# Gating the expert weights with the token index innermost: products on VectorE, and stored gates transposed and scaled by ScalarE

## What is computed

```python
q = (x_blk @ w_query).reshape(b, t, PEER_HEADS, 2, HALF_KEY)
scores = einsum('bthcd,hcnd->bthcn', q, sub_keys)
top_s, top_i = top_k(scores, PEER_TOPK)
...
gate = softmax(best_s)
u = expert_u[expert_idx]
v = expert_v[expert_idx]
act = gelu(einsum('btd,bthkd->bthk', x_blk, u), approximate=False)
out = einsum('bthk,bthkd->btd', gate * act, v)
```

## Time and profile before

| | before |
|---|---|
| median of the three runs | 1621.19 us |
| lowest, highest | 1617.91, 1624.16 us |
| the profiled execution: time | 1617.6 us |
| its span, first to last instruction | 1615.8 us |
| TensorE matmuls busy | 1460.4 us (90%) |
| GpSimd busy | 951.7 us (59%) |
| VectorE busy | 906.1 us (56%) |
| ScalarE busy | 744.1 us (46%) |

### The profile page before, as it was taken

The page is one execution under the profiler, slowest core; times in us unless marked ns, Lnnn a source line. Parts: engine busy times, 40 slices in busy tenths (PEclk is TensorE's granted clock), DMA queues, the critical chain, the costliest instruction groups (busy, mean ns, idle before and its releaser), DMA issues.

```text
span 1615.8 us, 22681 instructions
## 1 busy us (share of the span) xinstructions
PE 1460.4 (90%) x8920; PEld 1272.1 (79%) x8920; DVE 906.1 (56%) x1521; ACT 744.1 (46%) x1356; POOL 951.7 (59%) x665
## 2 busy tenths in 40 slices
PE   0699899869999599979998998999999999999998
PEld 0378566759988589657998998999998777778886
DVE  4464689245521487642379285777765787842222
ACT  2144212256544466534454555444444554555554
POOL 0063000336766364215689999876665999987675
PEclk8798555689999799989999999999999999999999
DMA  7434225225455243203544544545555566555552
GB/s 267 178 131 165 96 105 205 82 75 177 171 186 194 84 157 105 79 26 131 208 161 157 186 177 163 183 165 174 176 174 197 209 226 231 215 187 204 183 190 97
DMA packets 48298, 261.65 MB, mean 162 GB/s; under 512 B 5440, under 2 KB 14016, under 8 KB 19008
## 3 DMA queue, kind: packets, MB, share of 16 engines
q1 hardware_dynamic: 37984, 249.58, 43.4%
q10 hardware_dynamic: 10208, 10.63, 1.9%
HBM read 250.75 MB, written 9.44 MB: 161 GB/s over the span
## 4 chain that ended last, share of the span: by engine, by line
PE 72%; DVE 11%; POOL 8%; ACT 3%; issue 2%; PEld 2%; DMA 1%; PEldq 1%; ACTq 0%; DVEq 0%
PE bank L689 32%; PE bank L721 20%; PE bank L1264 17%; POOL v_lo L1746 7%; PEld bank L721 2%; DVE ada L1871 2%; PE bank L1050 1%; DMA arena<-pos_dram 1%; ACT arena L1320 1%; DVE arena L1871 1%; POOL v_lo L1738 1%; DVE arena L2296 1%; DVE x L1838 1%; PE bank L798 1%; DVE arena L1836 0%
## 5 line engine op out<-in xcount | busy, mean ns | idle before, releaser
L1746 POOL TENSOR_TENSOR v_lo<-ring,v_hi 128x512 fp32r<-128x512 f32 x448 | 658.4, 1485 | 155.3 <-ACT v_hi L1676 144.5
L1738 POOL TENSOR_TENSOR v_lo<-ring,d_hi 128x512 fp32r<-128x512 f32 x213 | 293.1, 1386 | 497.9 <-ACT d_hi L1362 434.6
L1676 ACT CAST v_hi<-ring 128x512 fp32r<-128x512 f32 x512 | 317.5, 621 | 393.4 <-PE bank L689 223.6
L689 PE MATMUL bank<-hT_hi,v_hi 128*128 128x256 f32 x1024 | 293.4, 287 | 8.7 <-POOL v_lo L1746 8.7
L689 PE MATMUL bank<-hT_lo,v_hi 128*128 128x256 f32 x1024 | 288.3, 282 | 0.0
L689 PE MATMUL bank<-hT_hi,v_lo 128*128 128x256 f32 x1024 | 286.7, 280 | 0.0
L1362 ACT CAST d_hi<-ring 128x512 fp32r<-128x512 f32 x236 | 143.5, 620 | 174.6 <-PE bank L721 139.8
L1264 PE MATMUL bank<-v_hi,mix_hi 128*128 128x512 f32 x512 | 206.3, 403 | 6.3 <-DVE mix_lo L2438 4.3
L689 PEld LDWEIGHTS bank<-hT_hi,v_hi 128*128 128x128 f32 x1024 | 194.5, 190 | 10.2 <-POOL v_lo L1746 8.2
L1264 PE MATMUL bank<-v_hi,mix_lo 128*128 128x512 f32 x512 | 200.9, 392 | 0.0
L1264 PE MATMUL bank<-v_lo,mix_hi 128*128 128x512 f32 x512 | 199.6, 390 | 0.0
(11 more groups left out here) (312 smaller groups left out, 2462.7 us busy)
## 6 DMA issues: line engine op xcount, KB each, us to landing
ring<-w_dram SPq DMA_DIRECT2D x228, 1024.0 KB, 4.8
gate_dram<-gput ACTq DMA_DIRECT2D x64, 128.0 KB, 2.4
gget<-gate_dram SPq DMA_DIRECT2D x32, 256.0 KB, 4.2
x<-x_dram SPq DMA_DIRECT2D x1, 1024.0 KB, 6.9
arena<-mem_dram ACTq DMA_DIRECT2D x1, 1024.0 KB, 8.3
out_dram<-x SPq DMA_DIRECT2D x1, 1024.0 KB, 4.0
arena<-const_dram ACTq DMA_DIRECT2D x1, 884.0 KB, 18.2
arena<-vec_dram ACTq DMA_DIRECT2D x1, 144.0 KB, 15.2
```

The costliest lines, as they stand in the source:

```text
L689: return nc.tensor.matmul(out_, lhsT, rhs, start=start, stop=stop)
L1676: nc.scalar.copy(v_hi[:, r, :], quarter(at, r)).then_inc(s_vhi, 1)
L1738: nc.gpsimd.tensor_tensor(v_lo[:, r, :], dense_quarter(d, r), d_hi[:, r, :], ALU.subtract).then_inc(s_dpl, 1)
L1746: nc.gpsimd.tensor_tensor(v_lo[:, r, :], quarter(at, r), v_hi[:, r, :], ALU.subtract).then_inc(s_plo, 1)
```

## The change

Three instructions get other access patterns; none is added, removed or moved, and the data are the same.

- `first_gated` walks position by position with the 4 tokens innermost. Before, it walked token by token with 64 positions innermost. In `area` the inner step goes from 1 KB to 4 bytes (4 neighbours, then a jump); in the bank it goes from 4 bytes to 512 bytes.
- The gate copy (ScalarE) reads the bank in the same new order, so `gput` holds position by position, 4 tokens each, and it multiplies by 1/GATE_UP. It reads the bank with an inner step of 512 bytes where it had 4.
- `second_gated` walks position by position with 8 tokens innermost (2 groups of 4 in `gget`), and is a plain tensor_tensor multiply, since the scale is already in. In `area` the inner step goes from 1 KB to 4 bytes; `gget` was read straight through and is now read in runs of 4, 1 KB apart in turn.

```diff
@@ second_gates(e), ScalarE
-                nc.scalar.copy(gput[:, e % 2, :].rearrange("p (t j) -> p t j", t=4),
-                               banks[2 + e % 2][:, :].rearrange("p (t j) -> p t j", t=4)[:, :, HD:P]
-                               ).then_inc(s_gcp, 1)
+                nc.scalar.mul(gput[:, e % 2, :].rearrange("p (j t) -> p j t", t=4),
+                              banks[2 + e % 2][:, :].rearrange("p (t j) -> p j t", t=4)[:, HD:P, :],
+                              1.0 / GATE_UP).then_inc(s_gcp, 1)
@@ first_gated(e), VectorE
-                w = half_weights(0)[:, 4 * e:4 * e + 4, :]
-                g = banks[2 + e % 2][:, :].rearrange("p (t j) -> p t j", t=4)[:, :, 0:HD]
+                w = area[1].rearrange("p (j t) -> p j t", t=T)[:, :, 4 * e:4 * e + 4]
+                g = banks[2 + e % 2][:, :].rearrange("p (t j) -> p j t", t=4)[:, 0:HD, :]
                 stt(w, g, 1.0 / GATE_UP, w, ALU.mult, ALU.mult).then_inc(s_gdr, 1)
@@ second_gated(k), VectorE
-                w = half_weights(1)[:, 8 * k:8 * k + 8, :]
-                g = gget[:, k % FETCH, :].rearrange("p (t j) -> p t j", t=8)
-                stt(w, g, 1.0 / GATE_UP, w, ALU.mult, ALU.mult).then_inc(s_gd2, 1)
+                w = area[0].rearrange("p (j t) -> p j t", t=T)[:, :, 8 * k:8 * k + 8].rearrange(
+                    "p j (g t) -> p j g t", g=2)
+                g = gget[:, k % FETCH, :].rearrange("p (g j t) -> p j g t", g=2, t=4)
+                tt(w, w, g, ALU.mult).then_inc(s_gd2, 1)
```

More of the change, by code:

```diff
@@ L614, in quarter @@
             return ring[:, n % RING, r * 512:(r + 1) * 512]
-        def half_weights(half):
-            return area[1 - half].rearrange("p (j t) -> p t j", t=T)
         NORMS = ["mem", "h1", "post1", "h2", "post2", "h3", "h4"]
```

## The result

The changed kernel took 1605.88 us in the median of four runs (1604.15 to 1607.79); the kernel before 1620.88 us, also in four (1617.91 to 1624.16). The ratio is 0.9908, with a 95% interval from 0.9887 to 0.9929: 15 us less, where 9.3 had been forecast. So the first thing to settle is what of the 15 us belongs to the change. The profiled execution after took 1604.18 us.

What follows compares the result with a forecast made beforehand. TensorE's matmuls cover 90% of the span; in 30 value tiles, alternating VectorE and GpSimd operations (5.78 us against TensorE's 5.49) bind. Terms -9.5 + 0 + 0.2 = -9.3 us, from 1621.2 to 1611.9 us; range 1606 to 1619.5.

Steps and rivals of the forecast that it cites:

- The product of the values: VectorE's product in the first 30 value tiles: 0.69 us instead of 1.29, saving 0.60 us for each of 32.
- rival B: Value product does not get faster; only the plainer kind saves, 0.06 us in 25 tiles, 1.5 us: 1619.9; chance 0.07.
- The turns: VectorE's and GpSimd's two-input operations alternate in product tiles; period 5.78 to 5.18 us, below TensorE's 5.49: -9.5 us.
- the long tiles: Value tiles 15 and 16, together losing 2.96 us, and 19, losing 1.32; rival A said they could stay long.
- Rivals A: Turns still bind: overlap shrinks, period 5.68 us, 4.7 of the 9.5 us stay lost: 1616.6; chance 0.17.
- The product beside the gates: VectorE's product in first_gated: 757 ns as before, both TensorE waits for one-hots stay, 0 us; ends 479 ns and 1.3 us.
- case E: Bank's step free: gates' product 479 ns, copy no longer, -11.0 us, 1610.2; counted with the forecast, 0.63 in all.
- The gate copy: ScalarE's copy from the bank: 0.23 us longer, only the last copy exposed, +0.2 us.
- Rivals C: Bank's step somewhat dear: copy 0.6 us longer, 20 groups stall 0.35 each, net -1.9 us, 1619.3; chance 0.08.
- D: Gate copy stalls TensorE before the gates of e+2; at 1.2 us growth +10.7 us, 1631.9; chance 0.05.

Runs made afterwards that it cites:

- doubled copy: Changed kernel with each gate copy preceded by one like it into unused memory; ratio 0.9926 (0.9906 to 0.9947) of the kernel before.
- repeated comparison: Changed kernel run again, no edit, beside the kernel before: 1608.01 us median of six runs against 1619.67 of 28, ratio 0.9933.

## Why the prediction came out as it did

- **The product of the values.** Forecast 0.69 us, measured 0.684. L2213 was the right row. The reading of L1871 was wrong: I took 0.06 us of its 752 ns for the kind, and the kind costs nothing. It changed no term; rival B's 1.5 us would have been zero. It did make the price of the 1 KB step too low, 1.06 ns an element for 1.19 (and 1.09 for 1.30 beside the gates).
- **The turns.** Forecast -9.5, measured -9.8 in the first 30 tiles and -10.0 over the stage. That the period would fall below TensorE's 5.49 us was right, and the long tiles went too. GpSimd's mean fell further than to my 1600 ns, to 1389; it meets VectorE less often, with 30 of 90 subtractions over 1.4 us where 75 of 89 had been. The size of the turn, 5.18 us, stays unproven: it can't be read where TensorE sets the pace, and the same sum is too long for a product of 1.08 us (5.58 us, where the tiles took 5.49 with GpSimd idle for 0.9). The gain did not depend on it, as anything below 5.49 gives the same. Rivals A and B fall.
- **The product beside the gates.** This is the term that was mis-sized: "I choose the middle, 757 ns as before: the bank's step costs what the SBUF step cost". It costs nothing: 424 ns. I had priced the bank by the only stepped row there was, and that was a row of SBUF. The term is -1.2 us by the two profiles and not 0, and between -0.3 and -2.0 by all of them; this is case E, whose -1.5 was taken from one execution's two stops. The product fell even below my lower end of 479 ns, because L1801 is not a straight copy of its form; what its 55 ns more are was not tested.
- **The gate copy.** Forecast 0.23 us longer and 0.2 us at the end of the chain; measured 11 ns longer, and 0.0. The step that failed is the same: "one more cycle for each of 256" for the bank's step, which costs ScalarE nothing. Rivals C and D had the right place, shown by the doubled copy, and no price to pay there.
- **The sum.** -10.0 - 1.2 + 0 is -11.2 by the traces, and E had said -11.0. The repeated comparison says 10.9.
- **The number and the range.** The forecast of 1611.9 missed the first median by 6.0 us: 1.9 by the terms, of which 1.4 are the bank's step (1.2 and 0.2) and 0.5 the values; 0.3 since the kernel before was itself 0.3 lower in its four runs than in three; and 3.8 by what the first comparison holds beyond the change. The failing step of the range is "1606, E with the runs' scatter": it allowed 4 us below E for scatter, and 4.3 were needed. The profile before had no more than three runs, 6 us apart, and medians of so few can both be off, in opposite directions: in the repeated comparison the kernel before was 1.2 us lower than in the first and the changed one 2.1 us higher. That median, 1608.01, lies inside the range. So the range was missed by no more than scatter makes, and the error in the working is the price of the bank's step, in both of its terms.

## What to carry to other kernels

Where the operations of two engines lengthen each other, as VectorE's with two SBUF inputs and GpSimd's do here, work out the length of one period and compare it with the pace of the engine that should bound: a saving counts down to that pace and no further. Adding up the lengths of both engines and subtracting the overlap that the trace shows tells on which side of that pace a clear case lies; within 0.1 us it told the wrong side here. Let the innermost count walk at least two neighbours in SBUF on both the reading and the writing side. When a change moves a step from one memory to another, do not price the second by the first; and when a forecast gain is of the size of the runs' scatter, give the range room for the scatter of two medians.

## What the runs showed that I had not expected

- A step of 512 bytes in a PSUM bank costs VectorE and ScalarE nothing that shows: 424 ns for 256 elements, below the 479 of the straight L1801, and 377 ns with the step and without. VectorE was not run in the same form on a straight bank. The Trainium skill, "Advanced Engine Details and Errata", section "Memory Cachelines", warns of non-contiguous PSUM patterns for matmuls; for these two engines the trace shows no such price.
- A 1 KB step in SBUF costs about 0.8 ns an element on one side and 1.2 to 1.3 on both; with two elements in a row it costs 0.08 ns an element (726 - 684 over 512).
- The stop of TensorE ahead of the values was followed by tile 0 at a mean granted clock of 0.76 or 0.78, between the two levels of 1.2 and 2.4 GHz; with the stop 0.78 us shorter the clock stayed at 2.4 GHz, which gave 1.4 us on top of the shorter stop. One execution shows this.
